# The first four modulation chunks: from shared sums on VectorE and TensorE to sums on TensorE alone, in four column groups

## The reference

```
mod = silu(c) @ w_ada + b_ada              # (1024) @ (1024, 6144): shift, scale, gate, ...
h   = rms_norm(x, g_mix)
h   = h * (1 + scale) + shift              # 512 tokens x 1024
latents = h @ w_in[:, :416]                # what the first attention starts from
```

## Time and profile before

| | |
|---|---|
| median of three executions | 2030.7 us (2026.68 to 2030.97) |
| profiled execution, span from first to last instruction | 2026.4 us; of its time outside the span nothing is given |
| TensorE matmul busy | 1950.7 us, 96% |
| VectorE busy | 986.1 us, 49% |
| ScalarE busy | 662.0 us, 33% |
| mean granted TensorE clock | 0.983 |

### The profile page before, as it was taken

One profiled execution on the slowest core, in us unless ns is written; L12 is line 12 of the kernel. 1 busy time (PEld: TensorE's weight loads), 2 busy tenths in 40 slices (PEclk: granted clock), 3 DMA queues, 4 the chain that ended last, 5 costly groups with the idle time before them and its releaser, 6 DMA issues.

```text
span 2026.4 us, 23969 instructions
## 1 busy us (share of the span) xinstructions
PE 1950.7 (96%) x9117; PEld 1353.6 (67%) x9117; DVE 986.1 (49%) x1865; ACT 662.0 (33%) x1238; POOL 162.7 (8%) x169
## 2 busy tenths in 40 slices
PE   7999899996999999988999999999999999999998
PEld 3478576673333334446888888888677888888886
DVE  6474545342122222584565555555256756555554
ACT  2572722241111112358432222232336633222222
POOL 1000000021111110204100000011000020000001
PEclk9999999997999999999999999999999999999999
DMA  9555134357999787110322322232440022232201
GB/s 320 191 141 189 61 130 161 143 184 281 418 397 361 287 328 264 42 42 1 120 88 83 104 105 83 103 105 92 165 156 1 1 84 83 89 119 83 90 35 42
DMA packets 104871, 292.55 MB, mean 144 GB/s; under 512 B 13445, under 2 KB 24403, under 8 KB 91712
## 3 DMA queue, kind: packets, MB, share of 16 engines
q1 hardware_dynamic: 92352, 266.60, 35.7%
q0 software_dynamic: 11408, 22.27, 3.5%
q10 hardware_dynamic: 1008, 2.29, 0.3%
HBM read 331.22 MB, written 24.69 MB: 176 GB/s over the span
## 4 chain that ended last, share of the span: by engine, by line
PE 87%; DVE 7%; DMA 2%; ACT 2%; issue 1%; ACTq 0%; DVEq 0%; SPq 0%; POOLq 0%
PE bank L1425 18%; PE bank L1427 17%; PE bank L1426 17%; PE bank L1821 8%; PE bank L1342 5%; PE bank L1847 4%; PE bank L1384 3%; PE bank L1410 2%; PE bank L1396 2%; PE bank L1877 1%; PE bank L1629 1%; PE bank L1805 1%; DVE top L3313 1%; PE bank L1416 1%; DVE hT L3314 1%
## 5 line engine op out<-in xcount | busy, mean ns | idle before, releaser
L3203 DVE TENSOR_TENSOR weights_low<-weight_ring,weights_high 128x1024 fp32r<-128x1024 f32 x128 | 159.1, 1243 | 264.5 <-ACT weights_high L2303 264.5
L1427 PE MATMUL bank<-hidden_high,weights_low 128*128 128x512 f32 x688 | 267.6, 389 | 0.0
L1425 PE MATMUL bank<-hidden_high,weights_high 128*128 128x512 f32 x624 | 242.7, 389 | 0.0
L1426 PE MATMUL bank<-hidden_low,weights_high 128*128 128x512 f32 x624 | 242.7, 389 | 0.0
L2303 ACT ACTIVATE weights_high<-weight_ring 128x1024 fp32r<-128x1024 f32 x128 | 135.6, 1059 | 321.1 <-PE bank L1427 321.1
L1425 PE MATMUL bank<-normed_high,weights_high 128*128 128x512 f32 x512 | 200.4, 392 | 0.2
L1426 PE MATMUL bank<-normed_low,weights_high 128*128 128x512 f32 x512 | 199.3, 389 | 0.0
L1427 PE MATMUL bank<-normed_high,weights_low 128*128 128x512 f32 x512 | 199.2, 389 | 0.0
L1821 PE MATMUL bank<-weight_ring,arena 128*64 128x512 f32 x464 | 171.3, 598 | 4.6 <-issue 2.7
L1427 PEld LDWEIGHTS bank<-hidden_high,weights_low 128*128 128x128 f32 x688 | 129.1, 188 | 26.7
L1426 PEld LDWEIGHTS bank<-hidden_low,weights_high 128*128 128x128 f32 x624 | 117.1, 188 | 24.4
(11 more groups left out here) (567 smaller groups left out, 3522.3 us busy)
## 6 DMA issues: line engine op xcount, KB each, us to landing
weight_ring<-in_w_up SPq DMA_DIRECT2D x16, 2048.0 KB, 8.7
weight_ring<-in_w_down SPq DMA_DIRECT2D x16, 2048.0 KB, 7.8
weight_ring<-in_w_gate SPq DMA_DIRECT2D x29, 1024.0 KB
weight_ring<-in_w_up SPq DMA_DIRECT2D x29, 1024.0 KB
weight_ring<-in_w_ada SPq DMA_DIRECT2D x12, 2048.0 KB, 12.9
weight_ring<-in_w_down SPq DMA_DIRECT2D x19, 1024.0 KB
hT<-in_w_down SPq DMA_DIRECT2D x19, 1024.0 KB
weight_ring<-in_w_in SPq DMA_DIRECT2D x7, 2048.0 KB, 14.5
```

What stands on the lines that cost most here:

```text
L1425: pe.matmul(dst, high, rhs_high, start=first, stop=False)
L1426: pe.matmul(dst, high, rhs_low, start=False, stop=False)
L1427: return pe.matmul(dst, low, rhs_high, start=False, stop=last)
L3203: dve.tensor_tensor(piece_half(w_lo, ch, q), piece_of(ch, q), piece_half(w_hi, ch, q).bitcast(F32), ALU.subtract).then_inc(s_wlo, 1)
```

## The change

The four first chunks are summed wholly by TensorE. The eight columns of silu(c) are spread into `silu_spread`, eight blocks of 128 x 32 whose first column is the silu column and whose other columns are zero. VectorE clears the buffer at its start and ScalarE writes the eight columns. Matmul `k` of a chunk writes 32 partitions of the bank, those of column group `k % 4`; so each of the four column groups sums two tiles, and the bank holds four rows of partial sums and zeros between them. ScalarE copies the whole bank (128 x 512) into `mod_acc`, and `mod_columns`, as for the later chunks, sums over partitions and turns in one step. VectorE's `mod_partial` remains for chunks 4 to 11 only. The order on TensorE is changed too: the first latent group, sum of chunk 3, the second latent group, sum of chunk 1, both turns, then the first half of the third latent group, and after it the second halves.

```diff
-MOD_PE = (4, 4, 0, 0)
-MOD_DONE = tuple(sum(KD - k for k in MOD_PE[:n + 1]) for n in range(len(MOD_PE)))
...
                 g = G[("mod", c)]
                 begin(g)
-                pe.wait_ge(s_macc, MOD_DONE[3] + KD * (n - 3))
+                if n < 4:
+                    g_read(pe, G[("mod_sum", c)])
+                else:
+                    pe.wait_ge(s_macc, KD * (n - 3))
...
-            def mod_row_sum(c, n, between=None):
+            def mod_quarter_sums(c):
                 g = G[("mod_sum", c)]
                 w = ws(W[("ada", c)], (KD, 512))
                 w_ready(pe, W[("ada", c)])
                 begin(g)
-                for k in range(MOD_PE[n]):
-                    pe.matmul(psum(g)[0:1, :], silu_c[:, k:k + 1], w[:, k, :], start=(k == 0), stop=False)
-                if between is not None:
-                    between()
-                pe.wait_ge(s_macc, MOD_DONE[n])
-                pe.matmul(psum(g)[0:1, :], ones[:, 0:1], mod_acc[:, n % 2, :], start=(MOD_PE[n] == 0), stop=True)\
-                    .then_inc(mm_done, 1)
+                for half in range(2):
+                    for n in range(4):
+                        k = 4 * half + n
+                        last = pe.matmul(psum(g)[32 * n:32 * n + 32, :], silu_spread[:, k, :], w[:, k, :],
+                                         start=(half == 0), stop=(half == 1), skip_group_check=True)
...
-            mod_row_sum(MOD_FIRST[0], 0, bias_and_vectors)
-            mod_row_sum(MOD_FIRST[1], 1)
+            mod_quarter_sums(MOD_FIRST[0])
+            bias_and_vectors()
+            mod_quarter_sums(MOD_FIRST[1])
             for n in range(2):
-                mod_row_turn(MOD_FIRST[n], n)
+                mod_columns(MOD_FIRST[n], n)
...
-            latents(0, 0, 2)
-            mod_row_sum(MOD_FIRST[2], 2)
-            latents(0, 2, 3)
-            mod_row_sum(MOD_FIRST[3], 3)
-            for n in range(2, 4):
-                mod_row_turn(MOD_FIRST[n], n)
-            latents(1)
+            latent(0, 0)
+            mod_quarter_sums(MOD_FIRST[2])
+            latent(0, 1)
+            mod_quarter_sums(MOD_FIRST[3])
+            mod_columns(MOD_FIRST[2], 2)
+            mod_columns(MOD_FIRST[3], 3)
+            latent(0, 2)
+            for m in range(3):
+                latent(1, m)
...
-            act.activation(rstd[0:1, 0:1], silu_c[0:1, 0:1], ACT.Copy).then_inc(s_cs, 1)
+            act.wait_ge(s_spread, 1)
+            act.activation(silu_spread[:, :, 0], silu_c[:, :], ACT.Copy).then_inc(s_cs, 1)
...
+            def mod_sums_out(n):
+                if n >= 2:
+                    act.wait_ge(mm_done, done(G[("mod", MOD_FIRST[n - 2])]))
+                evac(G[("mod_sum", MOD_FIRST[n])], mod_acc[:, n % 2, :])
...
+            dve.memset(silu_spread, 0.0).then_inc(s_spread, 1)
...
-            mod_partial(MOD_FIRST[0], 0, MOD_PE[0], KD)
...
-            mod_partial(MOD_FIRST[1], 1, MOD_PE[1], KD)
             first_modulation(0)
             over_root(4, KD)
-            mod_partial(MOD_FIRST[2], 2, MOD_PE[2], KD)
-            mod_partial(MOD_FIRST[3], 3, MOD_PE[3], KD)
             first_modulation(1)
```

More of the change, by code:

```diff
@@ L192, in plan @@
     group("norm_mix")
[L193 to L198, removed]
+    for n, c in enumerate(MOD_FIRST):
+        group(("mod_sum", c))
+        if n == 0:
+            group("toe1")
+            group("vec")
+        if n % 2 == 1:
+            group(("mod", MOD_FIRST[n - 1]))
             group(("mod", c))
@@ L444, in two_block_kernel @@
         s_cs = sem("silu_c_ready")
+        s_spread = sem("silu_spread_cleared")
         s_c = sem("c_loaded")
@@ L673, in psum @@
             return bank[g % BANKS]
-        mod_acc, c_in, mod_row = ar(14336, 2, T), ar(11392, P, rows=KD), ar(13312, 2, T, rows=1)
+        mod_acc, c_in, silu_spread = ar(14336, 2, T), ar(11392, P, rows=KD), ar(13312, KD, 32)
         table1, table1_T = ar(11520, 513, rows=H), ar(12048, 3 * H)
@@ L1621, in _, with latent @@
             g = G["lat"]
[L1623 to L1632, removed]
-            latents(0, 0, 2)
-            mod_row_sum(MOD_FIRST[2], 2)
-            latents(0, 2, 3)
-            mod_row_sum(MOD_FIRST[3], 3)
-            for n in range(2, 4):
-                mod_row_turn(MOD_FIRST[n], n)
-            latents(1)
+            def latent(half, m):
+                if not half:
+                    begin(g + m)
+                for k in range(4 * half, 4 * half + 4):
+                    pe.wait_ge(s_h, k + 1)
+                    last = pe.matmul(psum(g + m)[:, :], w[:, k, m * P:m * P + P], hT[:, k, :], start=(k == 0),
+                                     stop=(k == KD - 1))
+                if half:
+                    last.then_inc(mm_done, 1)
+            latent(0, 0)
[7 more added lines that the diff above has]
+                latent(1, m)
             g = G["kr"]
@@ L2366, in _ @@
             evac(g, table1_T[:, :], psum(g)[:, 0:3 * H])
+            def mod_sums_out(n):
+                if n >= 2:
+                    act.wait_ge(mm_done, done(G[("mod", MOD_FIRST[n - 2])]))
+                evac(G[("mod_sum", MOD_FIRST[n])], mod_acc[:, n % 2, :])
+            mod_sums_out(0)
             g = G["toe1"]
@@ L2380, in rope_tables @@
                     act.activation(table[rows, :], arg[rows, :], ACT.Sin).then_inc(s_trig, 1)
[L2382 to L2386, removed]
             def modulated(half):
@@ L2396, in modulated @@
                                    bias=modT[:, j:j + 1]).then_inc(s_h, 1)
-            mod_row_out(0)
-            mod_row_out(1)
+            mod_sums_out(1)
             modulated(0)
-            mod_row_out(2)
-            mod_row_out(3)
+            mod_sums_out(2)
+            mod_sums_out(3)
             modulated(1)
@@ L2807, in mod_partial @@
             def mod_partial(c, n, k0, k1):
-                first = MOD_PE[n] if n < 4 else 0
-                if k0 == first and n >= 2:
-                    dve.wait_ge(mm_done, done(G[("mod", n - 2)] if n >= 6 else G[("mod_sum", MOD_FIRST[n - 2])]))
+                if k0 == 0:
+                    dve.wait_ge(mm_done, done(G[("mod", n - 2 if n >= 6 else MOD_FIRST[n - 2])]))
                 w_ready(dve, W[("ada", c)])
@@ L2815, in mod_partial @@
                 for k in range(k0, k1):
-                    if k == first:
+                    if k == 0:
                         ins = dve.tensor_scalar(acc, w[:, k, :], silu_c[:, k:k + 1], None, ALU.mult)
```

## The result

| | before | after |
|---|---|---|
| median, us | 2029.9 (7 runs, 2020.57 to 2030.97) | 2017.21 (7 runs, 2014.24 to 2019.05) |
| ratio to before | 1 | 0.9942 [0.993, 0.9954] |
| profiled execution: span, us | 2026.4 | 2015.2 |
| its own time, us | see the table of before | 2016.89 |
| VectorE busy, us (instructions) | 986.1 (1865) | 968.9 (1842) |

The change makes the kernel faster by 11.8 us (9.3 to 14.2) by the ratio; the medians stand 12.7 us apart. The direction and the place were right, the size was not.

What follows compares the result with a forecast made beforehand. TensorE, busy 96% of the span, was taken as the bound. Gains of 5.3, 1.4 and 1.9 us less 1.6 given back made 7.1 us: 2030.7 to 2023.6 us, range 2018.5 to 2028.

Steps and rivals of the forecast that it cites:

- sums 1.85: First four chunks on TensorE: each sum, eight 32-column matmuls in four column groups, takes 1.85 us.
- latents begin 8.1 us on: Behind the first two sums and turn: latents begin at 29.84 us, 5.3 us earlier than before.
- first latent group 5.21: First eight latent records on TensorE: slow clock kept as before, 5.21 us against 3.41 at full clock.
- `kr` 36.3 us on: Start of `kr` behind the latents: at 58.05 us where it was 65.11, a gain of 7.1 us.
- (b): At the sums: switches of tiling mode drain the array, 4.7 us in all; gain 3.4 us, 2027.3 us; chance 0.04.
- (c): At the sums: column groups do not overlap, 6.8 us a sum; 12.4 us slower, 2043.1 us; chance 0.03.
- Rival (a): After the turns at 42.4 to 44.3: the clock falls again, price 1.8 us; gain 5.3, 2025.4 us; chance 0.31.
- the tenth or two that the forecast allowed: Around each sum on TensorE: 0.1 us for entering the mode, and 1.93 us to the sum's end.
- What is earlier there is earlier at the end: Behind `kr`: all that follows is released by work, not a clock, so its 7.1 us carries to the end.
- Rival (d): Later, say the wait at 161.86 or other clock falls: gain given back, 0 to 3 us left, 2029; chance 0.14.
- the fall at 54 us: In the second latents: no slow clock follows the covered modulation, 12.26 us becomes 10.3, worth 1.9 us.
- The forecast's base: Whole kernel: median before of 2030.7 us, from three runs 4.3 us apart, less 7.1 gives 2023.6.

Runs made afterwards that it cites:

- experiment 4: Kernel after with all eight matmuls of a chunk in one group of 32 columns, not four: 2039.55 us, ratio 1.0051 to the kernel before.
- Experiment 5: One-column matmuls added in TensorE's idle start: 20 in the kernel before, 2026.26 us (ratio 0.9984); 44 in the kernel after, 2019.33 us (0.9953).
- padded kernels: Kernel before with 20 one-column TensorE matmuls more, 2026.26 us; kernel after with 44 more, 2019.33 us; both in idle time, moving the instruction list.
- experiment 1: Both kernels run again with no edit: before 2028.26 us (ratio 1.000), after 2018.19 us (0.9943).
- experiment 8: Kernel after with 23 small VectorE memsets more, 2017.93 us; kernel before with only the change's memset and semaphore added, 2036.99 us (ratio 1.0044).
- experiment 6: Kernel after with two useless matmuls filling TensorE's wait between the first turn and first latents, run twice: 2014.47 us (0.9931) and 2015.42 us (0.9936).
- experiment 7: Kernel after in the old TensorE order, with two useless matmuls between the second turn and second latents: 2020.32 us, ratio 0.9959 to the kernel before.
- kernel with more memsets: Kernel after with 23 small memsets more on VectorE before its first wait: 2017.93 us, one round.
- experiment 2: Kernel after with latents and sums in the old order of the kernel before: 2020.94 us, ratio 0.9963 to the kernel before.
- padded kernel after: Kernel after with 44 one-column TensorE matmuls more in idle time at the start: 2019.33 us, ratio 0.9953 to the kernel before.

## Why the prediction was right and wrong

**Right, term by term, up to `kr`.** Forecast and measured from the first sum: sums 1.85 and 1.85; latents begin 8.1 us on, 8.0; first latent group 5.21, 5.19; `kr` 36.3 us on, 36.2; gain 7.1, 7.2. The sum of each chunk stands where the earlier trace rows put it from L1645, the vectors had landed when asked for (L1578 follows directly on the first sum), SP's issues at L992 went out at 22.84, and no load kept TensorE waiting. ScalarE's wider copy took 0.60 us. Rivals (b) and (c) are excluded by the 1.85 us, and experiment 4 shows that (c) had very nearly the right price (6.98 for 6.8). Rival (a), to which I had given 0.31, did not happen in either profile of the kernel after (granted 1.00 from 44 to 62 us).

The Trainium skill, "TensorEngine Tiling (Array Packing)", Key Properties, has a change of tiling mode drain the engine. Here the chain shows 1.85 us a sum with the next instruction directly behind, so a drain costs at most the tenth or two that the forecast allowed.

**Wrong: "What is earlier there is earlier at the end."** This step took `kr` for the whole. It left out three things, all of one sign here:

1. The load of chunk 6. The forecast let the 8.99 us of the earlier trace rows "move along with it" unchanged. It became 8.0. Experiment 5 shows the cause in both directions: the change lengthens TensorE's list by 80 entries, and a packet of it that was fetched beside the load comes at another time. By itself 1.0 us; the padded kernels moved by 3.3 and 1.9 us in all, so that the change with the list held in place is worth 8.0 or 9.4 us. Rival (d) named this wait, with the opposite sign.
2. The clock at other places. From the mean granted clock (0.9817 and 0.9835) the time at 1.2 GHz is 2 x (1 - clock) x span: 74.3 us a run before (72 runs) and 66.5 after (12 runs). At half speed this is 3.9 us, of which 1.9 is the fall at 54 us that the sum held. The other 2.0 us were not in it. The falls behind 430 us are not tied to the change's stage; each differs between executions of one kernel. That the mean went down with the change is measured, but not every pair of profiles shows it (experiment 1); why it did is not shown.
3. 0.36 us outside the span, of unknown cause (experiment 8).

7.2 + 1.0 + 2.0 + 0.36 = 10.6 of the 11.4 us between the means. The rest, 0.8, is near the standard error of that difference (0.6). The sum is a bookkeeping from two profiles and the mean clocks; the terms were not each isolated, and items 1 and 2 are not independent, since a load that lands later also moves where TensorE idles.

The forecast's base was off as well: 2030.7, the median of three runs, where 72 runs average 2029.1. That is 1.6 of the 6.4 us between 2023.6 and 2017.2; from the mean the range would have begun at 2016.9.

The forecast's range failed for the same reason: it let later effects take the gain away, 0.14 for (d), but gave them no chance to add to it. A mirror of (d) was due: the two padded kernels, experiment 6 and the memset of experiment 8 show shifts of 3.3 down, 1.9 up, 2.3 down and 8 up from edits that cost TensorE next to nothing.

The term for the first latents, 5.21 us "as before", was right in these two profiles and still not safe: behind the same bare wait the clock fell in the kernel after, its repeat, experiment 7 and the kernel with more memsets, and not in experiment 2 nor in the padded kernel after.

## What to carry to other kernels

Matmuls that use 32 columns each can be laid beside each other in four column groups (3.8 times here), and here a reduction that TensorE does wholly then beat one shared with VectorE, above all since it could be put where it covers a wait. If a stage's gain is worked out exactly, do not take it for the gain of the kernel: look for what in the later waits depends on alignment (a packet of instructions beside a load, which of two engines starts first, the clock), and widen the range to both sides by some 3 us for a kernel of 2 ms. To see what a change itself is worth, compare it also with a kernel before whose list is padded to the same length. Where TensorE must wait a microsecond or two ahead of a long stretch of matmuls, it can be worth trying to give it work that nobody needs: it brought about 2 us in experiment 6, and nothing in experiment 7.

## What the runs showed of the hardware

- A 2 MB load was issued in the kernel before and landed 8.94 to 9.45 us later with one 16 KB instruction packet among its own in four of five profiles that had one, and 7.78 to 8.15 without (nine profiles). In the four it came 4.9 to 6.8 us after the issue. The fifth had it 7.2 us after the issue and landed in 7.92.
- The same VectorE operation on 128 x 1024 took 1.23 us when it began 0.06 us ahead of GpSimd's twin, and 2.67 us when it began 0.30 us behind it.
- The bare wait of 1.4 to 1.5 us behind a pair of turns was followed by a granted clock of 0.50 in 15 of 17 cases, and the same wait filled with two matmuls in none of three.
- One wait of 1.6 us on TensorE was followed by 17 us at the lower clock, and the two cost 9.4 us in that profile.
- Sixteen records of 32 columns took 1.85 us in four groups and 6.98 in one.
